# The first half of the out-projection of the sparse attention in quarters between the pairs of heads

## What is computed

```
c_q, k, v, k_idx, w_idx = split(h @ w_in)
q, q_idx = heads of rms_norm(c_q) @ w_uq, @ w_uq_idx
score[q, key] = sum over 8 index heads of w_idx * relu(q_idx . k_idx), masked by blocks
keep the 128 best keys of each query
p = softmax(q . k over the kept keys), 16 heads of 64
o = p @ v
x = x + o @ w_out           (1024 x 1024)
```

## Time and profile before

| | us |
|---|---|
| median of 3 runs | 2345.7 |
| lowest and highest | 2344.35, 2346.25 |
| the profiled execution, its own time | 2347.26 |
| its span in the profile | 2345.5 |
| PE busy | 2314.8 (99%) |
| DVE, ACT, POOL busy | 790.0, 853.2, 1176.2 |
| mean granted clock of TensorE | 0.998 |

### The profile page before, as it was taken

The page is one execution under the profiler, slowest core; times in us unless marked ns, Lnnn a source line. Parts: engine busy times, 40 slices in busy tenths (PEclk is TensorE's granted clock), DMA queues, the critical chain, the costliest instruction groups (busy, mean ns, idle before and its releaser), DMA issues.

```text
span 2345.5 us, 26852 instructions
## 1 busy us (share of the span) xinstructions
PE 2314.8 (99%) x11076; PEld 1883.8 (80%) x11076; DVE 790.0 (34%) x1368; ACT 853.2 (36%) x1258; POOL 1176.2 (50%) x982
## 2 busy tenths in 40 slices
PE   8999999999999999999999999999999999999999
PEld 7888888888977888888887688888887757888887
DVE  4222204864223222201457652022046854210310
ACT  4322214514343332213447543123156464421330
POOL 5544445635654544444551374444456943554442
PEclk9999999999999999999999999999999999999999
DMA  4332323312332332322220132232321202323322
GB/s 150 97 101 90 108 90 100 101 55 90 126 108 72 96 102 90 108 90 92 88 91 19 55 105 93 92 106 90 101 93 58 87 1 66 97 90 107 91 90 90
DMA packets 147584, 209.61 MB, mean 89 GB/s; under 512 B 7259, under 2 KB 113926, under 8 KB 147462
## 3 DMA queue, kind: packets, MB, share of 16 engines
q1 hardware_dynamic: 147462, 207.89, 27.5%
HBM read 205.77 MB, written 2.10 MB: 89 GB/s over the span
## 4 chain that ended last, share of the span: by engine, by line
PE 89%; DVE 7%; issue 2%; POOL 1%; ACT 1%; DMA 0%; SPq 0%; DVEq 0%; POOLq 0%; ACTq 0%
PE ps L1534 28%; PE ps L1536 27%; PE ps L1535 27%; DVE c_work L3065 1%; DVE c_best L3064 1%; DVE small L2908 1%; POOL wlo L795 1%; PE ps L2339 1%; PE ps L1873 1%; PE ps L2310 1%; PE ps L1895 1%; PE ps L2320 1%; POOL sq L810 0%; PE ps L2264 0%; PE ps L1980 0%
## 5 line engine op out<-in xcount | busy, mean ns | idle before, releaser
L795 POOL TENSOR_TENSOR wlo<-raw,whi 128x512 fp32r<-128x512 f32 x772 | 1004.0, 1333 | 977.6 <-ACT whi L1015 952.6
L1015 ACT ACTIVATE whi<-raw 128x2048 fp32r<-128x2048 f32 x184 | 350.6, 1905 | 630.6 <-DMA raw<-in_mlp_w 303.6
L1534 PE MATMUL ps<-hh,whi 128*128 128x512 f32 x1448 | 569.0, 393 | 2.7 <-DVE hl L2479 2.5
L1536 PE MATMUL ps<-hh,wlo 128*128 128x512 f32 x1448 | 564.2, 390 | 0.0
L1535 PE MATMUL ps<-hl,whi 128*128 128x512 f32 x1448 | 564.1, 390 | 0.0
L1534 PEld LDWEIGHTS ps<-hh,whi 128*128 128x128 f32 x1448 | 272.1, 188 | 62.6 <-issue 6.2
L1535 PEld LDWEIGHTS ps<-hl,whi 128*128 128x128 f32 x1448 | 272.2, 188 | 56.9 <-issue 1.2
L1536 PEld LDWEIGHTS ps<-hh,wlo 128*128 128x128 f32 x1448 | 272.1, 188 | 57.0
L1534 PE MATMUL ps<-gh,whi 128*128 128x512 f32 x736 | 286.3, 389 | 0.0
L1535 PE MATMUL ps<-gl,whi 128*128 128x512 f32 x736 | 286.3, 389 | 0.0
L1536 PE MATMUL ps<-gh,wlo 128*128 128x512 f32 x736 | 286.3, 389 | 0.0
(11 more groups left out here) (457 smaller groups left out, 2846.7 us busy)
## 6 DMA issues: line engine op xcount, KB each, us to landing
raw<-in_mlp_w SPq DMA_DIRECT2D x64, 1024.0 KB, 5.5
raw<-in_ffn_w_up SPq DMA_DIRECT2D x22, 1024.0 KB, 5.1
raw<-in_ffn_w_down SPq DMA_DIRECT2D x22, 1024.0 KB, 4.8
raw<-in_ffn_w_gate SPq DMA_DIRECT2D x21, 1024.0 KB, 5.1
raw<-in_w_in SPq DMA_DIRECT2D x12, 1024.0 KB, 5.2
raw<-in_diff_w_in SPq DMA_DIRECT2D x12, 1024.0 KB, 5.0
raw<-in_xattn_w_kv SPq DMA_DIRECT2D x8, 1024.0 KB, 5.0
raw<-in_dsa_w_in SPq DMA_DIRECT2D x8, 1024.0 KB, 5.0
```

The source lines that it names most:

```text
L795: nc.gpsimd.tensor_tensor(wlo[i][:, c], raw[i][:, c], whi[i][:, c].bitcast(F32), ALU.subtract).then_inc(s_lo, 1)
L1015: nc.scalar.activation(whi[i][:, 0:width(made[0])], raw[i][:, 0:width(made[0])], ACT.Copy)\
L1534: nc.tensor.matmul(dst, w_hi, x_hi, start=start, stop=False)
L1536: return nc.tensor.matmul(dst, w_lo, x_hi, start=False, stop=stop)
```

## The change

The first half of each output tile is cut in two. `first_quarter(p)` runs k = 0 and 1, six products into bank 7, at eight steps named by `FIRST_QUARTER`; `second_quarter(n)` runs k = 2 and 3, six products, where `first_half(n)` stood. Each quarter is added to xT by DVE on its own, so there are eight additions more. Waits on the new semaphore `s_quart` keep bank 7 in order. The first quarter needs b+12 and heads 0 to 3 at p = 9, so ACT makes the high parts of b+12 to b+14 two steps earlier (p = 3 to 14 in place of 5 to 16), and POOL makes the low parts behind `out_parts` 0, 1 and 2 in place of 1, 2 and 3. The semaphore `s_frow` of the differential attention goes; `s_fsq` counts its event. The last products are issued by a function of their own, `second_half`, in the same order as before.

```diff
+FIRST_QUARTER = (9, 13, 14, 15, 17, 18, 22, 26)
+def out_pieces(p):
+    quarters = sum(q <= p for q in FIRST_QUARTER)
+    halves = max(0, (p - 17) // 2)
+    return quarters + halves - halves // 4
...
                 for j in range(8):
                     inverse_rows(j)
                     out_parts(j)
-                    if 1 <= j < 4:
-                        split_to(b + DSA_BLOCKS + j - 1)
+                    if j < 3:
+                        split_to(b + DSA_BLOCKS + j)
...
-                    if 5 <= p < 17:
-                        prep_part(b + 12 + (p - 5) // 4, (p - 5) % 4)
+                    if 3 <= p < 15:
+                        prep_part(b + 12 + (p - 3) // 4, (p - 3) % 4)
...
-                        r.then_inc(s_frow, 1)
+                        r.then_inc(s_fsq, 1)
...
                     if j < 3:
                         pe.wait_ge(s_rtc, 32 + 2 * j)
+                    if j == 3:
+                        pe.wait_ge(s_quart, 4)
...
+                    if k == 34:
+                        pe.wait_ge(s_quart, 1)
...
-                                k % 4 == 0, k % 4 == 3)
+                                k == ks[0], k == ks[-1])
...
-                def first_half(n):
+                def first_quarter(p):
+                    n = FIRST_QUARTER.index(p)
                     bb = b + DSA_BLOCKS + n // 4
                     use(bb)
+                    if n == 0:
+                        pe.wait_ge(s_chl, 2)
+                    pe.wait_ge(s_cc, 33 + p // 4 - 1)
+                    if n:
+                        pe.wait_ge(s_quart, n)
+                    if p > 20:
+                        pe.wait_ge(s_x, 8 * upd + (p - 18) // 2)
+                    out_tile(bb, n, (0, 1), 7).then_inc(s_oh, 1)
+                def second_quarter(n):
...
                     if n == 0:
                         pe.wait_ge(s_chl, 4)
                     if n < 7:
                         pe.wait_ge(s_cc, 33 + (15 + 2 * n) // 4)
+                    pe.wait_ge(s_quart, min(8, 6 + n // 2))
                     if n:
                         pe.wait_ge(s_x, 8 * upd + n)
-                    out_tile(bb, n, range(4), 7 if n < 7 else 0)\
+                    out_tile(bb, n, (2, 3), 7 if n < 7 else 0)\
                         .then_inc(s_used if n % 4 == 3 else s_oh, 1)
...
+                    if p in FIRST_QUARTER:
+                        first_quarter(p)
                     if p >= 19 and p % 2 == 1:
-                        first_half((p - 19) // 2)
+                        second_quarter((p - 19) // 2)
...
+                def add_quarter(p):
+                    n = FIRST_QUARTER.index(p)
+                    dve.wait_ge(s_oh, out_pieces(p))
+                    V.scalar_tensor_tensor(out=xT[:, n, :], in0=ps[:, 7, :], scalar=1.0, in1=xT[:, n, :],
+                                           op0=ALU.mult, op1=ALU.add).then_inc(s_quart, 1)
...
+                    if p in FIRST_QUARTER:
+                        add_quarter(p)
                     if p >= 19 and p % 2 == 1:
                         add_half((p - 19) // 2)
```

More of the change, by code:

```diff
@@ L454, in two_blocks @@
         s_fsq = sem("s_fsq")
-        s_frow = sem("s_frow")
+        s_quart = sem("s_quart")
         s_fcopy = sem("s_fcopy")
@@ L2370, in out_tile, with second_half @@
                         r = mm3(ps[:, bank, :], whi[w][:, c], wlo[w][:, c], o_h[:, k, :], o_l[:, k, :],
-                                k % 4 == 0, k % 4 == 3)
+                                k == ks[0], k == ks[-1])
                     return r
-                def first_half(n):
+                def second_half(n, k):
+                    c = slice(k % 4 * S + n * P, k % 4 * S + n * P + P)
+                    w = (b + 14) % NBUF
+                    return mm3(ps[:, n, :], whi[w][:, c], wlo[w][:, c], o_h[:, k, :], o_l[:, k, :], k == 4, k == 7)
+                def first_quarter(p):
+                    n = FIRST_QUARTER.index(p)
                     bb = b + DSA_BLOCKS + n // 4
                     use(bb)
+                    if n == 0:
[7 more added lines that the diff above has]
+                def second_quarter(n):
+                    bb = b + DSA_BLOCKS + n // 4
                     if n == 0:
@@ L2410, in dsa @@
                 pe.wait_ge(s_cs, 64)
-                first_half(7)
+                second_quarter(7)
                 use(b + 14)
@@ L2415, in dsa @@
                     for n in range(4):
-                        out_tile(b + 14, n, (k,), n)
+                        second_half(n, k)
                 pe.wait_ge(s_chl, 8)
                 for n in range(4):
-                    out_tile(b + 14, n, (7,), n).then_inc(s_used if n == 3 else s_down, 1)
+                    second_half(n, 7).then_inc(s_used if n == 3 else s_down, 1)
                 pe.wait_ge(s_cpTa, 32)
@@ L2891, in diff @@
                     if g == 0:
-                        dve.wait_ge(s_frow, 1)
+                        dve.wait_ge(s_fsq, 6)
                         V.tensor_copy(rstd[:, :], ps[:, 6, :]).then_inc(s_fcopy, 1)
@@ L3114, in add_half @@
                     else:
-                        dve.wait_ge(s_oh, n - n // 4 + 1)
+                        dve.wait_ge(s_oh, out_pieces(19 + 2 * n))
+                    dve.wait_ge(s_quart, min(8, 6 + n // 2))
                     V.scalar_tensor_tensor(out=xT[:, n, :], in0=ps[:, 7 if n < 7 else 0, :], scalar=1.0,
                                            in1=xT[:, n, :], op0=ALU.mult, op1=ALU.add).then_inc(s_x, 1)
+                def add_quarter(p):
[3 more added lines that the diff above has]
+                                           op0=ALU.mult, op1=ALU.add).then_inc(s_quart, 1)
                 mask_min(0)
```

## The result

The changed kernel takes 2355.0 us (median of 5 runs, 2354.85 to 2355.44) where the one before takes 2345.7 (5 runs beside it, 2344.35 to 2347.23). The ratio is 1.0038, with a 95% interval of 1.0027 to 1.005: slower by 0.4%.

What follows compares the result with a forecast made beforehand. PE, busy 99% of the span, was taken as the bound, with at most 3.8 us of waits to fill. Stalls, quarters and shorter halves gave +6.5, the clock +2.4: 2345.7 + 8.9 = 2354.6 us, range 2349 to 2359.5.

Steps and rivals of the forecast that it cites:

- The first wait for c_inv: PE at turn_inverse(1): c_inv(1) stands behind POOL's split, which waits for ACT's last high part; stall of +3.4 us.
- The first quarter: PE at p = 9: it waits for o_l(1), 1.3 us with the handing over, then runs the quarter, 1.5.
- turn_inverse(2): PE waits for c_inv(2) behind the split of b+13: shift +8.3 us, a stall of 3.3.
- turn(15): PE after quarters 13 and 14, which add 3.0 us and swallow the 1.29 wait: shift +10.0 before the clock.
- turn_inverse(3): PE waits for c_inv(3), which needs ACT's part of p = 14: shift +11.9 us before the clock.
- turn(19): PE after quarters 17 and 18, which add 3.0 us and swallow 0.77: shift +14.1 before the clock.
- The clock: TensorE's granted clock falls behind the two new stalls: 1.2 us each, +2.4 us; upper bound 1.6 each.
- DVE's additions: Eight additions of 0.69 us on DVE, costed at nothing; bound 0.3 us behind quarter 15.
- ACT's parts: Two parts of 0.5 us, new at p = 3 and 4, land in and before ACT's gap: nothing, at most 0.2 us.
- The wait at p = 31: Placed by the prediction at p = 30: ACT's copy is late behind a shorter run, half hidden; +0.4 us.
- Rival 2: POOL between p = 6 and 8: the splits hide and the quarters fill waits; -0.8 us, 2344.9; chance 0.08.
- Rival 4: PE at p = 10 to 16: quarters only push ACT's chain and swallow no waits; 2355; chance 0.07.

Runs made afterwards that it cites:

- the first two experiments: First: changed kernel, POOL makes c_inv before splitting a weight block, 2344.49 us. Second: kernel before, with only the weight-block preparation moved earlier, no quarters, 2362.33 us.
- the fourth: Changed kernel with ACT's high parts of b+12 to b+14 two more steps earlier, p = 1 to 12, POOL's order kept; 2344.99 us.
- the run with the quarter at 12: Changed kernel with POOL's c_inv before the weight-block split, and the first quarter moved from p = 9 to p = 12; 2344.35 us.
- the blocks alone: Kernel before, with only ACT's parts two steps earlier and POOL's splits one pair of heads earlier, no quarters; 2362.33 us.
- c_inv ahead of the split: Changed kernel with POOL spreading the next pair's reciprocals before it splits a weight block, not behind; 2344.49 us.
- the products in the wait: Changed kernel with 13 unread products into bank 7 ahead of each wait for c_inv(1) and c_inv(2); 2351.95 us.
- the other banks: Changed kernel with c_inv before the split, first quarter at p = 12, and tiles n = 6 and 7 in banks 1 and 4, not 7 and 0; 2342.0 us.
- the parts earlier: Changed kernel with ACT's high parts of b+12 to b+14 at p = 1 to 12 in place of 3 to 14; 2344.99 us.
- the six quarters: Changed kernel with c_inv before the split, first quarter at p = 12, banks 1 and 4, and no quarters at p = 22 and 26; 2342.01 us.

## Why the prediction was right

The forecast was 2354.6 and the measured median 2355.0; the difference to the kernel before was to be +8.9 and is +9.3. By the steps, with 1.13 added to each time of the changed kernel:

- **The first wait for c_inv.** Forecast for turn_inverse(1): 1888.9. Measured 1887.78 + 1.13 = 1888.91. The step from ACT's last part over the split's 4.9 to c_inv holds within 0.1 us, since each term came from a row of the same instruction. That these waits, and not the quarters, are the loss is shown by the first two experiments and the fourth.
- **The first quarter.** Wait forecast 1.3, measured 1.14; the run with the quarter at 12 shows that the net price was 0.3.
- **turn_inverse(2)**: forecast +8.3 without the clock, +9.5 with 1.2 for one fall; measured 1905.39 + 1.13 - 1896.73 = +9.8. **turn(15)**: +12.4 with two falls, measured +13.0. **turn_inverse(3)**: +14.3, measured 1921.15 + 1.13 - 1907.36 = +14.9 (the forecast's 1919.2 - 1907.36 is 11.8, where it has 11.9). Its own wait was to be 0.6, from 1918.6 to 1919.2, and is 0.94. **turn(19)**: +16.5, measured +17.0. Behind it PE got back what the shorter halves give: to the second half the shift falls to 1975.84 + 1.13 - 1967.78 = +9.2.
- **The clock** was the term that was mis-sized: 1.2 us for each fall, and the changed kernel's rows give 1.65, 3.3 in place of 2.4. My cap of 1.6, half of a slow stretch of 3.26 us, does not hold: the blocks alone show 1.7, 1.6 and 2.7, and behind the third wait `weigh` alone lost 1.5 us and the turning ahead of it 0.5. The forecast is nearer than its terms. Without the two falls the shift at the second half is 9.2 - 3.3 = 5.9 us, where the sum had 6.5; 0.9 too little for the clock and 0.6 too much for the rest cancel in part. That they do is luck. The Trainium skill's warning about bursts behind idle gaps ("TensorE: Matmul & The Clock Gate", "HAM oscillation — how this bites in real kernels") was the right one to follow here: all five waits over 3 us, two in the changed kernel and three with the blocks alone, were followed by a stretch at 1.2 GHz.
- **DVE's additions** show no cost, as said. The group of the eight new ones in the changed kernel names nobody who waited for them:

```profile
L3158 DVE SCALAR_TENSOR_TENSOR xT<-ps,xT x8: 692/692/692, 1896.2 to 1956.4; 128x512 f32<-128x512 f32 x8
```

- **ACT's parts** at p = 3 and 4 cost nothing, though one takes 0.62 us and not the 0.5 of the forecast: from turn(3) to scores(10) the changed kernel takes 1883.15 - 1869.37 = 13.78 us and the one before 1884.29 - 1870.50 = 13.79. The wait at p = 31 was forecast 0.4 and is 0.28.
- **Rival 2**, the splits that hide, is what the first and fourth experiments build: the forecast for it was -0.8, measured -1.5 and -1.5 in the distance. Part of the difference is that the filled waits are worth more than their brackets, since the modelled end of the work ahead covers 0.1 to 0.2 us of each: by starts, turn(11) came 1892.82 - 1891.46 = 1.36 us behind the start of the chunk's transposes, and in the changed kernel 1898.43 - 1897.94 = 0.49, which is 0.87 less for a bracket of 0.70. The rest of the difference was not taken apart.
- **Rival 4** named 2355, the measured number, and was wrong in its mechanism: the quarters did swallow the waits, as the missing brackets show. The number alone could not have told it from the forecast.

## What to carry to other kernels

When work on an engine with strict order is moved ahead of a small step, ask when its last input comes, and not how long it runs: here a copy of 0.6 us stood behind a split that waited 3.9 us for its input. Two moves that belong together, producer and consumer, must move by the same distance, or the slack between them must be counted. And put the step that others wait for ahead of the bulk: this alone took 10.5 us off, and left a time that can't be told from that of before.

## What the runs showed of the hardware

A wait of 3.6 to 3.7 us of PE was followed by a fall of the clock all five times, and the fall costs 1.6 to 1.7 us more than the wait itself in four of them and 2.7 in one. Idle time filled with products that nobody reads gives most of that back: 26 products made the kernel 3 us faster.

Behind a shorter wait the clock fell in some executions and not in others. The wait of 1.92 us (1.94 in the changed kernel) stands in all nine traces of this case, and a fall follows it in six (the kernel before, the changed one, c_inv ahead of the split, the blocks alone, the products in the wait, the other banks) and none in three (the parts earlier, the first quarter at 12, the six quarters), though the instructions ahead of it are the same. First before, then the first quarter at 12, which is 2 us earlier at this place, so that the stretch holds the whole of it in both:

```profile
1726.00:1740.00 14.00, 12.08 (x66) 11.34 (x65) 3.42 (x5) 5.98 (x19) 9.61 (x8) 0.88 0.19 62
```

```profile
1726.00:1740.00 14.00, 11.87 (x66) 10.31 (x65) 3.42 (x5) 6.18 (x27) 9.36 (x9) 1.00 0.27 91
```

A second place of this kind lies near 1324, in the differential attention. Its longest wait is 0.97 us in all nine traces, and the clock fell there in three (the kernel before, the parts earlier, the six quarters). The span less the distance, which is the part of the program that no edit touches, goes with the count of falls at these two places: 2227.3 us with none (the first quarter at 12), 2228.6 to 2229.9 with one (seven traces), 2230.3 with both (the kernel before). So such falls are likely a part of the 3 us by which the runs of one kernel differ. No run was made to set this apart, and 1.3 us among the traces with one fall stay open.
